# Values stationary on two column groups in two attentions of a transformer trunk kernel

## What is computed

```python
# a: 4 heads, 512 queries, 768 keys (512 tokens + 256 context), values of 64
p = softmax(q0 @ k0.T) - lam * softmax(q1 @ k1.T);  o = p @ v      # then rmsnorm per head
# b: 4 heads, the same shapes, one softmax with a bias on the 512 token keys
p = softmax(q @ k.T + bias);                        o = p @ v
```

## Time and profile before

| | us |
|---|---|
| median of 3 runs | 1329.33 |
| lowest, highest | 1328.54, 1332.23 |
| profiled execution | 1334.26 |
| its span (first to last instruction) | 1332.2 |
| TensorE busy, its clock over the span | 1220.0, 0.954 |
| DVE busy | 862.2 |
| ScalarE busy | 588.6 |
| attention a, about | 286 to 378 us of the span |
| attention b, about | 378 to 444 us |

### The profile page before, as it was taken

One profiled execution on the slowest core, in us unless ns is written; L12 is line 12 of the kernel. 1 busy time (PEld: TensorE's weight loads), 2 busy tenths in 40 slices (PEclk: granted clock), 3 DMA queues, 4 the chain that ended last, 5 costly groups with the idle time before them and its releaser, 6 DMA issues.

```text
span 1332.2 us, 16908 instructions
## 1 busy us (share of the span) xinstructions
PE 1220.0 (92%) x6412; PEld 899.1 (67%) x6412; DVE 862.2 (65%) x1282; ACT 588.6 (44%) x781; POOL 129.2 (10%) x126
## 2 busy tenths in 40 slices
PE   6999999968799995899999999889999898989996
PEld 1444474857688764788888888648877777765774
DVE  3479788768775447588898888664337555734543
ACT  1540010335555524487777787343333443334422
POOL 1101101000122000011221111300000000000000
PEclk9999999988799997899999999999999899899998
DMA  8735656770130053699999999652343445544301
GB/s 360 279 134 221 237 234 224 182 158 1 56 147 1 0 201 136 237 359 392 408 411 398 408 409 401 247 197 78 110 172 108 145 169 155 167 144 157 126 0 63
DMA packets 52822, 267.52 MB, mean 201 GB/s; under 512 B 15031, under 2 KB 22071, under 8 KB 38040
## 3 DMA queue, kind: packets, MB, share of 16 engines
q1 hardware_dynamic: 38264, 205.85, 42.1%
q0 software_dynamic: 9744, 47.19, 9.8%
q10 hardware_dynamic: 4752, 13.63, 2.7%
HBM read 226.80 MB, written 36.70 MB: 198 GB/s over the span
## 4 chain that ended last, share of the span: by engine, by line
PE 74%; DVE 13%; ACT 5%; DMA 3%; issue 3%; SPq 2%; POOL 1%; DVEq 0%; ACTq 0%; POOLq 0%
PE PS L2772 21%; PE PS L3196 7%; PE PS L3197 7%; PE PS L3198 7%; PE PS L3110 3%; PE PS L3422 3%; PE PS L3423 3%; PE PS L3424 3%; PE PS L3328 2%; PE PS L3327 2%; PE PS L3329 2%; PE PS L3064 2%; PE PS L3408 1%; SPq L804 1%; PE PS L2789 1%
## 5 line engine op out<-in xcount | busy, mean ns | idle before, releaser
L1394 ACT ACTIVATE arena_r<-ring 128x2048 fp32r<-128x2048 f32 x100 | 185.9, 1910 | 11.7 <-ACT arena L1431 7.4
L2772 PE MATMUL PS<-arena 128*128 128x64 f32 (+6 forms) x674 | 150.1, 390 | 30.0 <-DMA arena<-in_small_f_w 7.6
L2223 DVE TENSOR_TENSOR arena_r<-ring,arena_r 128x2048 fp32r<-128x2048 f32 x66 | 148.2, 2286 | 20.3 <-ACT arena_r L1394 19.7
L2772 PEld LDWEIGHTS PS<-arena 128*128 128x128 f32 (+2 forms) x674 | 100.2, 205 | 73.9 <-issue 40.5
L2772 PE MATMUL PS<-hT,ring 128*128 128x512 f32 (+1 forms) x304 | 118.9, 549 | 0.0
L3196 PE MATMUL PS<-arena_r,hT_r 128*128 128x512 f32 x272 | 112.4, 413 | 4.9 <-DVE hT_r L2405 4.9
L3422 PE MATMUL PS<-arena_r 128*128 128x512 f32 x256 | 104.7, 409 | 13.0 <-DVE ring_r L2631 8.5
L3197 PE MATMUL PS<-arena_r,hT_r 128*128 128x512 f32 x272 | 108.9, 400 | 0.0
L3424 PE MATMUL PS<-arena_r,ring_r 128*128 128x512 f32 x256 | 101.8, 398 | 0.0
L1203 ACT ACTIVATE arena<-PS 128x1024 f32<-128x1024 f32 (+2 forms) x31 | 28.5, 927 | 159.7 <-PE PS L2772 144.7
L2772 PEld LDWEIGHTS PS<-hT,ring 128*128 128x128 f32 x304 | 57.1, 190 | 59.0 <-issue 57.4
(11 more groups left out here) (481 smaller groups left out, 2416.0 us busy)
## 6 DMA issues: line engine op xcount, KB each, us to landing
ring<-in_moe SPq DMA_DIRECT2D x51, 2048.0 KB, 10.5
ring<-in_slabs SPq DMA_DIRECT2D x27, 2048.0 KB, 8.9
ring<-in_slabs SPq DMA_DIRECT2D x9, 1024.0 KB, 5.5
y_rows<-arena ACTq DMA_DIRECT2D x16, 512.0 KB, 10.0
ssm_scratch<-arena POOLq DMA_DIRECT2D x4, 1152.0 KB, 5.1
arena<-ssm_scratch POOLq DMA_DIRECT2D x4, 1152.0 KB, 8.3
ssm_scratch<-arena POOLq DMA_DIRECT2D x4, 1024.0 KB, 10.9
y_rows<-in_tab_no_token SPq DMA_DIRECT2D x1, 4096.0 KB, 25.1
```

Source lines behind the costliest of these rows:

```text
L1394: nc.scalar.activation(rounded(moe_w_hi[n][:, cols]), ring[:, n, cols], ACT.Copy).then_inc(s_moe_hi[n], 1)
L2223: nc.vector.tensor_tensor(rounded(moe_w_lo[n][:, cols]), ring[:, n, cols], as_float(moe_w_hi[n][:, cols]), ALU.subtract).then_inc(s_moe_lo ...
L2772: ins = nc.tensor.matmul(out, lhsT, rhs, start=(n == 0), stop=(n == len(pairs) - 1))
```

## The change

The product o is replaced by V `("v", i)`: the value tile (128 keys x 64) is stationary and the transposed probabilities (128 keys x 128 queries) move. Even key tiles go to the columns 0 to 63 of the array, odd ones to 64 to 127, so the result is two partial sums, one below the other, transposed. ScalarE copies this 128x128 block to `o_T`. A product with `o_T` stationary and two stacked 64x64 identities (`halves_sum`, one DVE addition at the start) moving turns it back and adds the halves. It is written behind the transposes of T, into the same unit's free columns: T(i) also makes the output of head i-2. The last two outputs have a unit of their own, `("o", n-1)`, at the end of each attention. ScalarE, not DVE, now scales and stores each output, after the copy of T and ahead of the one signal for both. DVE keeps the reciprocal (in b `root_sum_b`), and one semaphore, `s_scaled`, tells ScalarE and TensorE of it.

```diff
@@ def turns(a, n):
         if behind:
-            yield ("o", i - 1)
+            yield ("v" if a != "g" else "o", i - 1)
...
+    if a != "g":
+        yield ("o", n - 1)
...
+def turned_in(a, i, n):
+    return (a, "t", i + 2) if i + 2 < n else (a, "o", n - 1)
+def outputs_in(kind, i, n):
+    if kind == "o":
+        return [n - 2, n - 1]
+    return [i - 2] if i >= 2 else []
@@ ScalarE
+            def outputs(a, key):
+                for m, o in enumerate(outputs_in(key[1], key[2], n)):
+                    qt, h = o // HEADS, o % HEADS
+                    act.wait_ge(s_scaled, o + 1 + (n if a == "b" else 0))
+                    dst = o_a[:, qt] if a == "a" else post[:, qt % 2]
+                    first = (TC if key[1] == "t" else 0) + VD * m
+                    ins = nc.scalar.activation(dst[:, VD * h:VD * h + VD], both(key)[:, first:first + VD], ACT.Copy,
+                                               scale=stat[:, (2 * o if a == "a" else 2 * n + o) % 8, 3:4])
+                return ins
...
-                        nc.scalar.activation(probT_a if a == "a" else probT_b, both(key)[:, 0:TC], ACT.Copy).then_inc(s_act_read, 1)
+                        ins = nc.scalar.activation(probT_a if a == "a" else probT_b, both(key)[:, 0:TC], ACT.Copy)
+                        if i >= 2:
+                            ins = outputs(a, key)
+                        ins.then_inc(s_act_read, 1)
...
-                    elif turn[0] == "o":
+                    elif turn[0] == "v":
+                        filled(act, key)
+                        nc.scalar.activation(o_T[:, i % 2], bank(key, 0)[:, 0:P], ACT.Copy).then_inc(s_act_read, 1)
                         if a == "a":
                             high_b(i)
+                    elif turn[0] == "o":
+                        filled(act, key)
+                        outputs(a, key).then_inc(s_act_read, 1)
@@ DVE
-                if i >= 1:
-                    output("a", i - 1)
...
+            then(nc.vector.tensor_tensor(halves_sum, ident[:, 0:VD], ident[:, VD:2 * VD], ALU.add))
...
-                output("b", i - 1)
+                root_sum_b(i - 1).then_inc(s_scaled, 1)
@@ TensorE
+            def outputs(a, key):
+                for m, o in enumerate(outputs_in(key[1], key[2], n)):
+                    read(pe, (a, "v", o))
+                    first = (TC if key[1] == "t" else 0) + VD * m
+                    ins = nc.tensor.matmul(both(key)[:, first:first + VD], o_T[:, o % 2], halves_sum, start=True, stop=True)
+                return ins
...
+                        if i >= 2:
+                            ins = outputs(a, key)
                         ins.then_inc(s_filled, 1)
-                    elif turn[0] == "o":
+                    elif turn[0] == "v":
                         start_unit(key)
                         read(pe, (a, "t", i))
                         h = i % HEADS
                         v, pT = (v_a, probT_a) if a == "a" else (v_b, probT_b)
-                        products(bank(key, 0)[:, 0:VD],
-                                 [(pT[:, P * t:P * t + P], v[:, t, VD * h:VD * h + VD]) for t in range(KT)], last=True)
+                        for t in range(KT):
+                            c = t % 2
+                            ins = nc.tensor.matmul(bank(key, 0)[VD * c:VD * c + VD, 0:P], v[:, t, VD * h:VD * h + VD],
+                                                   pT[:, P * t:P * t + P], start=(t < 2), stop=(t >= KT - 2))
+                        ins.then_inc(s_filled, 1)
+                    elif turn[0] == "o":
+                        start_unit(key)
+                        outputs(a, key).then_inc(s_filled, 1)
```

More of the change, by code:

```diff
@@ L133, in unit_of @@
         turn = turn[0:2]
-    return (a, *turn), ("dve" if kind == "o" else "act")
+    return (a, *turn), ("dve" if kind == "o" and a == "g" else "act")
+def turned_in(a, i, n):
[4 more added lines that the diff above has]
+    return [i - 2] if i >= 2 else []
 def units_of_block_one():
@@ L374, in two_blocks @@
         k_hi_b, k_lo_b = region(R_FWD, [2, TC]), region(R_FWD + 2 * TC, [2, TC])
+        o_T, halves_sum = rstd[:, 0:2 * P].rearrange("p (a b) -> p a b", a=2), rstd[:, 2 * P:2 * P + VD]
         o_a = region(R_QKV + 1024, [QT, 256])
@@ L624, in two_blocks @@
         s_max = sem("s_max")
-        s_prob = sem("s_prob")
+        s_scaled = sem("s_scaled")
         s_o = sem("s_o")
@@ L1330, in _ @@
                         if turn[1] == 1:
-                            filled(act, ("a", "o", n - 1))
+                            filled(act, ("a", "v", n - 1))
                         nc.scalar.activation(prob_b[turn[1]], both(key)[:, 0:TC], ACT.Exp, bias=stat[:, j % 8, 0:1], scale=1.0,
@@ L1337, in _ @@
                         if i >= 1:
-                            filled(act, (a, "o", i - 1))
+                            filled(act, (a, "v", i - 1))
                         elif a == "b":
-                            filled(act, ("a", "o", n - 1))
-                        nc.scalar.activation(probT_a if a == "a" else probT_b, both(key)[:, 0:TC], ACT.Copy).then_inc(s_act_read, 1)
+                            filled(act, ("a", "v", n - 1))
+                        ins = nc.scalar.activation(probT_a if a == "a" else probT_b, both(key)[:, 0:TC], ACT.Copy)
+                        if i >= 2:
+                            ins = outputs(a, key)
+                        ins.then_inc(s_act_read, 1)
                         if a == "b":
@@ L2109, in combine, with root_sum_b @@
                 nc.vector.scalar_tensor_tensor(out=prob_a[:, i % 2, 0], in0=prob_a[:, i % 2, 1], scalar=stat[:, j + 1, 3:4],
[L2110 to L2130, removed]
+                                               in1=prob_a[:, i % 2, 0], op0=ALU.mult, op1=ALU.add).then_inc(s_scaled, 1)
+            def root_sum_b(i):
+                j = (2 * n + i) % 8
+                read(dve, ("b", "s", i, 0))
+                return nc.vector.reciprocal(stat[:, j, 3:4], stat[:, j, 1:2])
             oh = o_a.rearrange("p a (b c) -> p (a b) c", b=HEADS)
@@ L3041, in out_tr @@
                 start_unit(key)
-                read(pe, ("b", "o", HEADS * qt + HEADS - 1))
+                read(pe, turned_in("b", HEADS * qt + HEADS - 1, n))
                 for c in range(2):
@@ L3058, in _ @@
                         if a == "a":
-                            pe.wait_ge(s_prob, i + 1)
+                            pe.wait_ge(s_scaled, i + 1)
                         else:
```

## The result

| | before | after |
|---|---|---|
| median of 5 runs, us | 1329.33 | 1342.20 |
| lowest, highest | 1319.66, 1333.59 | 1339.72, 1344.22 |
| profiled execution, its span | 1334.26, 1332.2 | 1343.95, 1342.1 |
| TensorE's clock over the span | 0.954 | 0.944 |
| ScalarE busy, DVE busy | 588.6, 862.2 | 601.3, 855.6 |

The change makes the kernel slower: ratio 1.0101, 95% interval 1.0055 to 1.0146. In later runs the kernel before had medians of 1331.89 (19 runs), 1332.75 (25) and 1335.02 (23), and against those after is 7 to 10 us longer; that is the likelier size, though after itself was timed beside the first five only.

The account below looks back on a forecast made before the run. The prediction took a loop through every engine to bound the second attention and mostly DVE the first. Terms 0.65 + 2.4 + 0.4 + 0.8 = +4.3 us on the 1329.33 median gave 1333.6, range 1327.5 to 1339.5.

Parts of the forecast that it names:

- V, T, S: In a head, V to T (transposes of probabilities) 0.80 us against 1.37; T to S (scores) end 2.35 against 2.07.
- the groups of 64: Rival, slower: V's two column groups do not run together, V takes 1.31 us, time 1340; chance 0.10.
- The loop, not TensorE's amount: Second attention: a loop through every engine sets the pace, two heads taking 7.17 us against 7.04 before.
- TensorE's pace: Rival, faster: TensorE's work sets the pace, each of 32 heads gains 0.2 us, time 1323.5; chance 0.12.
- The seam: Between the attentions: late last outputs delay mean_a, T's copy comes 2.6 us later, TensorE idles about 2.7; +2.4 us.
- The cheaper seam: Rival: the seam between the attentions costs less than reckoned, time 1330.5 without 3 us of it; chance 0.16.
- Attention a: First attention: output copies, turning product between T and S0, and the addition at the start sum to +0.65 us.
- Steady b: Second attention, steady state: +0.8 us for 12 heads, less 0.4 where TensorE is the bound for two heads: +0.4.
- End of b: End of the second attention: last transposes at 444.7 against 443.91 from the same T(15) start, +0.8 us.
- the clock at the seam: Rival, slower: TensorE's 2.7 us idle between the attentions lowers its clock, +2 to 3 us, time 1336; chance 0.17.

Follow-up runs that it names:

- the change in b alone: V and the turning product in the second attention only, the first attention as in the kernel before: 1333.83 us, ratio 0.9997 to before.
- the old kernel with the late wait: Kernel before, with mean_a on DVE made to wait until the last convolution piece is filled: 1361.37 us, ratio 1.0198 to before.
- the kept-busy kernel: Changed kernel plus 10 useless products on TensorE ahead of the scores of the second attention's head 2: 1331.05 us, ratio 0.9984 to before.
- the useless products: Changed kernel plus 11 useless products at the second attention's V(0), where they waited for a PSUM slot: 1337.99 us, ratio 1.0046 to before.
- outputs ahead: Changed kernel with the first attention's last two outputs moved ahead of the last convolution piece: 1333.10 us, ratio 0.9981 to before.
- the two with useless products: Changed kernel with 10 useless products ahead of head 2's scores, or 11 at V(0), in the second attention: 1331.05 and 1337.99 us.

## Why the prediction was right and wrong

The direction was right. The forecast was 8.6 us too low, and 1342.2 lies above the range.

- **V, T, S.** V to T 0.80 forecast, 0.80 measured; the groups of 64 run together, and that rival is out. At 1.2 GHz it is 398.97 - 397.49 = 1.48 against the old product's 419.22 - 416.61 = 2.61 (the old kernel with the late wait). T to T at full clock 7.17 forecast, 7.09 measured, mostly because T to the end of the scores takes 418.00 - 415.71 = 2.29 instead of 2.35. (Two slips of the working change nothing: the output copy of 0.32 less 0.1 is 0.22, not 0.24, and the 1.34 us of product in one sentence is 1.37 by the row.)
- **The loop, not TensorE's amount, bounds b.** With ScalarE's copies and the turning product in the loop it is 7.09, with both out of it 6.45. The rival "TensorE's pace" would have made the change in b alone faster; it is 0.9997.
- **The seam.** Forecast: `mean_a` to start at 383.0, T's copy at 385.9, TensorE 2.7 us idle, +2.4. Measured: 382.91, 385.76, 2.60, +2.77 for T(1). The cheaper seam is out.
- **Attention a.** Forecast +0.65, of it +0.45 at T(14). Measured from the first T of a, T(14) is +0.43 and T(0) of b +0.22; the addition at the start is not to be seen. Over-estimated by some 0.4.
- **Steady b.** Forecast +0.4; from T(5) to T(11), at full clock in both, it is 8.29 - 8.73 = -0.4. Small, and of the other sign: argued, not tested, TensorE is the bound for more heads than the two that I counted, where the turning of a's result and the pool's products stand.
- **End of b.** Forecast 4.67 us from T(15) to the last transposes; the kept-busy kernel, at full clock there, has 4.62. In after it was 6.10, because it fell in a low stretch. The forecast had no wait of 1.95 us for V(14) ahead of it.
- **The step that failed: the clock at the seam.** I had the mechanism, gave it a chance of 0.17 as a rival and priced it at +2 to 3 us, from the 10 us at 1.2 GHz of the earlier trace rows. It came in all four profiled executions in which TensorE idled 2 us or more there, and in after it cost +6.0 behind the seam; the second low stretch, at the end of b, cost 1.4 more than the forecast there. The size was off since the low stretch of 20.5 us was twice the one I read, and each of its heads lost 2 us. The chance was off since I treated as a hazard what followed from my own forecast: I predicted 2.7 us of idle time with a row in hand in which 2.22 us had been followed by the low clock. The traces had more of them: in attention a TensorE waits 2.2 or 3.3 us behind each of the two spectra, and in all eleven profiles both waits were met by the low clock, within the wait or up to 2.6 us behind it, for 3.4 to 17.1 us. The forecast and that rival should have been one case.

In sum, from the table of differences: attention a -0.02 (0.65 forecast), seam +2.77 (2.4), low clock behind it +5.98 (0), steady b -0.44 (+0.4), T(11) to T(15) with before's own low stretch -1.28 (0), end of b +2.22 (0.8), the rest of the span +0.7 (0): +9.9 measured, +4.3 forecast.

**What stays open.** Why the low stretch ends after 6.8 us with the useless products, after 20.5 with V in the loop and after 54.6 or 58 with the old product: TensorE is recorded as busy for nearly all of each (10.00 of 10 us and 20.00 of 20 us in the rows above). And what sets the low stretch at the end of b. The five kernels in which ScalarE reads V in b all wait 1.95 us for V(14) and 1.20 us for V(15); the clock fell there in three (after, b alone, outputs ahead) and not in the two with useless products. So the new loop adds a hazard of its own at its end, which the experiments at the seam do not settle. Nor does a fall need such a wait: before fell at 423.6, and in the 20 us ahead of that its longest wait was 0.52 us.

## What to carry to other kernels

When an edit moves the last piece of a stage's result, list what waits for that piece before counting what the edit saves; here one unit behind 3.7 us of products cost more than 32 cheaper products gave. Count the clock in: where the kernel's own trace shows such idle times followed by the low clock, price a new one of 2 us or more as the low clock over the heads behind it, and where the wait can't go, useless products in the gap are cheaper (2.4 us of them gave back 11 us in one kernel and 25 in the other). And give a new copy out of PSUM to the engine that is waiting at that point of the loop, and keep a new product off the loop's path too: here the two together made 7.09 us into 6.45.

## What the runs showed of the hardware

- An idle time of 2.0 to 2.6 us on TensorE went over into 1.2 GHz, within it or up to 1.3 us behind it, in all four kernels that had it at the seam (low for 20.5, 6.8, 58.0 and 54.6 us); 0.3 to 0.9 us there did not, in the others. In attention a waits of 2.2 and 3.3 us did, 22 of 22; waits of 1.95 us at the end of b did in three kernels of five.
- The low clock can outlast 40 us of an engine recorded as 100% busy (20.00 of 20.00 us twice, at 0.50). A busy share in the trace does not tell that the clock comes back.
- One wait of 2 us can decide between two paces for nine heads: with the old product the loop is the bound at 2.4 GHz (3.5 us a head), TensorE at 1.2 GHz (6.25 us).
- Two column groups of 64 run together: 12 instructions of 128 columns over 64 stationary ones in 0.80 us with the change of division, where 12 of 64 columns over 128 take 1.37 and the forecast for one after another was 1.31.
